# Expert products that read 128 stationary columns where 96 hold tokens

## The reference

```python
def swiglu(h, w1, w3, w2):
    return (jax.nn.silu(h @ w1) * (h @ w3)) @ w2

def moe_swiglu(h, router_w, router_b, w1, w3, w2):
    logits = h @ router_w + router_b
    top_val, top_idx = lax.top_k(logits, 2)
    top_p = jax.nn.softmax(top_val, axis=-1)
    combine = jnp.sum(one_hot(top_idx, 8) * top_p[..., None], axis=-2)
    out = 0
    for e in range(8):
        out = out + combine[..., e:e+1] * swiglu(h, w1[e], w3[e], w2[e])
    return out
```

## Time and profile before

| | |
|---|---|
| median of 3 runs | 2208.56 us (2206.45 to 2208.92) |
| the profiled execution | 2208.2 us, of which the profile's span is 2206.4 us |
| expert stage, first product to last | 1174.3 to 2188.4 us |
| its matmuls | 112 steps x 36 = 4,032 |
| granted clock of TensorE, mean | 0.978 |

### The profile page before, as it was taken

One profiled execution on the slowest core, in us unless ns is written; L12 is line 12 of the kernel. 1 busy time (PEld: TensorE's weight loads), 2 busy tenths in 40 slices (PEclk: granted clock), 3 DMA queues, 4 the chain that ended last, 5 costly groups with the idle time before them and its releaser, 6 DMA issues.

```text
span 2206.4 us, 27500 instructions
## 1 busy us (share of the span) xinstructions
PE 2115.6 (96%) x10750; PEld 1577.5 (71%) x10751; DVE 1121.6 (51%) x1293; ACT 1060.9 (48%) x1163; POOL 1274.9 (58%) x466
## 2 busy tenths in 40 slices
PE   5999999989999998999999999999999999999997
PEld 3875767548787886867986677777767677776775
DVE  2146021140100104354336877878787787888776
ACT  4235411133222124244325766666676666667665
POOL 2300422025445454303406999898989989898996
PEclk8999999989999998999998999999999999999999
DMA  7346323122222222263456999999899999989993
GB/s 301 117 173 267 117 79 131 55 98 77 96 96 95 96 77 96 77 253 147 192 214 232 363 345 345 343 344 363 332 351 345 345 342 345 364 331 353 345 344 135
DMA packets 69640, 503.16 MB, mean 228 GB/s; under 512 B 7744, under 2 KB 7872, under 8 KB 9088
## 3 DMA queue, kind: packets, MB, share of 16 engines
q1 hardware_dynamic: 68976, 497.92, 60.2%
q0 software_dynamic: 528, 3.41, 0.4%
HBM read 500.24 MB, written 1.05 MB: 227 GB/s over the span
## 4 chain that ended last, share of the span: by engine, by line
PE 50%; POOL 33%; issue 12%; ACT 2%; DMA 1%; DVE 1%; SPq 0%; POOLq 0%; ACTq 0%; DVEq 0%
POOL moe_lo L494 32%; PE bank L788 12%; PE bank L789 12%; PE bank L790 12%; PE bank L803 7%; PE bank L820 2%; DMA start_slab<-in_w_mod 1%; PE turned L995 1%; PE pv_bank L1013 1%; POOL w_lo L458 1%; PE bank L971 1%; PE bank L832 1%; ACT PR L1463 0%; ACT H_NEW L1394 0%; POOL HID_LO L726 0%
## 5 line engine op out<-in xcount | busy, mean ns | idle before, releaser
L494 POOL TENSOR_TENSOR moe_lo<-moe_slab,moe_hi 128x512 fp32r<-128x512 f32 x336 | 916.1, 2751 | 163.4 <-ACT moe_hi L1585 162.1
L494 DVE TENSOR_TENSOR moe_lo<-moe_slab,moe_hi 128x1536 fp32r<-128x1536 f32 x336 | 688.4, 2054 | 174.9 <-ACT moe_hi L1585 172.6
L458 POOL TENSOR_TENSOR w_lo<-slab,w_hi 128x2048 fp32r<-128x2048 f32 (+3 forms) x72 | 295.4, 4105 | 678.2 <-ACT w_hi L1351 678.1
L1585 ACT ACTIVATE moe_hi<-moe_slab 128x2048 fp32r<-128x2048 f32 x336 | 629.4, 1906 | 0.1
L788 PE MATMUL bank<-moe_hi,HE_HI 128*96 128x512 f32 x896 | 360.2, 402 | 1.4 <-POOL moe_lo L494 1.4
L790 PE MATMUL bank<-moe_hi,HE_LO 128*96 128x512 f32 x896 | 353.0, 394 | 0.0
L789 PE MATMUL bank<-moe_lo,HE_HI 128*96 128x512 f32 x896 | 351.8, 393 | 0.0
L788 PE MATMUL bank<-H_HI,w_hi 128*128 128x512 f32 (+1 forms) x880 | 325.3, 370 | 17.6 <-POOL H_LO L692 12.6
L789 PE MATMUL bank<-H_LO,w_hi 128*128 128x512 f32 (+1 forms) x880 | 321.6, 365 | 0.0
L790 PE MATMUL bank<-H_HI,w_lo 128*128 128x512 f32 (+1 forms) x880 | 321.0, 365 | 0.0
L1351 ACT ACTIVATE w_hi<-slab 128x2048 fp32r<-128x2048 f32 (+1 forms) x72 | 135.4, 1883 | 161.1 <-PE bank L790 146.3
(11 more groups left out here) (202 smaller groups left out, 2435.8 us busy)
## 6 DMA issues: line engine op xcount, KB each, us to landing
moe_slab<-in_moe_up SPq DMA_DIRECT2D x224, 1024.0 KB, 4.8
moe_slab<-in_moe_w SPq DMA_DIRECT2D x112, 1024.0 KB, 4.9
slab<-in_w_in SPq DMA_DIRECT2D x38, 1024.0 KB, 4.8
slab<-in_ffn_w SPq DMA_DIRECT2D x30, 1024.0 KB, 4.7
slab<-in_w_mod SPq DMA_DIRECT2D x20, 1024.0 KB, 5.4
side_slab<-in_w_mod SPq DMA_DIRECT2D x20, 1024.0 KB, 8.4
start_slab<-in_w_mod SPq DMA_DIRECT2D x8, 1024.0 KB, 17.6
slab<-in_w_proj SPq DMA_DIRECT2D x8, 1024.0 KB, 6.9
```

Source lines behind the costliest of these rows:

```text
L458: engine.tensor_tensor(lo, raw, hi.bitcast(F32), ALU.subtract).then_inc(done, 1)
L494: engine.tensor_tensor(moe_lo[n][:, blocks, :], moe_slab[k % MOE_RING][:, blocks, :], moe_hi[n][:, blocks, :].bitcast(F32), ALU.subtract). ...
L1585: af(moe_hi[k % MOE_SPLIT][:], moe_slab[k % MOE_RING][:], ACT.Copy).then_inc(moe_hi_ready, 1)
```

## The change

The matmuls of the expert products now load 128 stationary columns instead of 96. The window starts where the chunk starts (SLOTS x chunk), so it takes in the chunk's 96 columns and 32 of what lies behind: columns of the next chunk, or, behind the last one, a pad of 32 (WIDE) columns. The result therefore fills all 128 rows of the PSUM bank. Rows 96 to 127 are read by nobody. Moving operands, number of matmuls, and their order stay as they are.

For this HE_HI, HE_LO, GE_HI and GE_LO get another layout, with a pad at the end of each half (HE: 4 chunks and a pad, twice for each expert; GE: 2 chunks and a pad). HE_LO moves to 138.5 KB, GE_HI and GE_LO to 160 and 162, OUT to 16 KB in the ring. The pads are filled with zeros once, by six operations on GpSimd ahead of its first low part of the stage; these wait for `last_turn`, since H and its neighbours lie there until then. TensorE waits for all six (`pads_ready`) behind the first gather. The copies that fill HE and GE handle the same elements in the new layout.

```diff
+WIDE = P - SLOTS
...
-        HE_HI = at("HE_HI", 132, [P, 2, DC, SLOTS], F32R)
-        HE_LO = at("HE_LO", 138, [P, 2, DC, SLOTS], F32R)
+        HE_HI, HE_LO = (at(n, kb_, [P, 2, 2, 4 * SLOTS + WIDE], F32R) for n, kb_ in (("HE_HI", 132), ("HE_LO", 138.5)))
...
-        GE_HI = at("GE_HI", 170, [P, 2, 2, SLOTS], F32R)
-        GE_LO = at("GE_LO", 171.5, [P, 2, 2, SLOTS], F32R)
+        GE_HI, GE_LO = (at(n, kb_, [P, 2, 2 * SLOTS + WIDE], F32R) for n, kb_ in (("GE_HI", 160), ("GE_LO", 162)))
...
-        OUT = at("OUT", 132, [P, DC, S])
+        OUT = at("OUT", 16, [P, DC, S])
...
+            pool.wait_ge(last_turn, 1)
+            for t in (HE_HI, HE_LO):
+                for he in range(2):
+                    nc.gpsimd.memset(t[:, he, :, 4 * SLOTS:].bitcast(F32), 0.0).then_inc(pads_ready, 1)
+            for t in (GE_HI, GE_LO):
+                nc.gpsimd.memset(t[:, :, 2 * SLOTS:].bitcast(F32), 0.0).then_inc(pads_ready, 1)
...
-                    ins = products(up[n % 2][0:SLOTS, :], (HE_HI[:, he, k, :], HE_LO[:, he, k, :]),
+                    ins = products(up[n % 2][:], [t[:, he, half, SLOTS * kk:SLOTS * kk + P] for t in (HE_HI, HE_LO)],
                                    [t[:, kk, :] for t in w], k == 0, k == DC - 1)
...
-                        ins = products(down[half][0:SLOTS, :], (GE_HI[:, n % 2, k, :], GE_LO[:, n % 2, k, :]),
+                        ins = products(down[half][:], [t[:, n % 2, SLOTS * k:SLOTS * k + P] for t in (GE_HI, GE_LO)],
                                        [t[:, 2 * k + half, :] for t in w],
...
             gather(0, (htok_act, htok_dve))
+            pe.wait_ge(pads_ready, 6)
             stream()
...
-                    af(HE_HI[:, he, 4 * b:4 * b + 4, :],
+                    af(HE_HI[:, he, b, 0:4 * SLOTS].rearrange("p (c n) -> p c n", c=4),
                        gath[b][:, 0:4 * SLOTS].rearrange("p (c n) -> p c n", c=4), ACT.Copy).then_inc(he_ready, 1)
```

More of the change, by code:

```diff
@@ L415, in build @@
         onehot_ready, gathered, he_ready = sem("onehot_ready"), sem("gathered"), sem("he_ready")
-        weighted_ready = sem("weighted_ready")
+        weighted_ready, pads_ready = sem("weighted_ready"), sem("pads_ready")
         last_turn, htok_act, htok_dve = sem("last_turn"), sem("htok_act"), sem("htok_dve")
@@ L1570, in turned_hidden @@
                 act.wait_ge(ge_turned, made)
-                af(GE_HI[:, n % 2, :, :], ge_bank[:, 0:2 * SLOTS].rearrange("p (m n) -> p m n", m=2), ACT.Copy)\
+                af(GE_HI[:, n % 2, 0:2 * SLOTS].rearrange("p (m n) -> p m n", m=2), ge_bank[:, 0:2 * SLOTS].rearrange("p (m n) -> p m n", m=2), ACT.Copy)\
                     .then_inc(ge_hi_ready, 1)
@@ L2060, in gathered_out @@
                     dve.wait_ge(he_ready, 2 * n + b + 1)
-                    v.tensor_tensor(HE_LO[:, he, 4 * b:4 * b + 4, :],
+                    v.tensor_tensor(HE_LO[:, he, b, 0:4 * SLOTS].rearrange("p (c n) -> p c n", c=4),
                                     gath[b][:, 0:4 * SLOTS].rearrange("p (c n) -> p c n", c=4),
-                                    HE_HI[:, he, 4 * b:4 * b + 4, :].bitcast(F32), ALU.subtract)\
+                                    HE_HI[:, he, b, 0:4 * SLOTS].bitcast(F32).rearrange("p (c n) -> p c n", c=4), ALU.subtract)\
                         .then_inc(he_lo_ready, 1)
@@ L2067, in turned_hidden @@
                 dve.wait_ge(ge_hi_ready, made)
-                v.tensor_tensor(GE_LO[:, n % 2, :, :], ge_bank[:, 0:2 * SLOTS].rearrange("p (m n) -> p m n", m=2),
-                                GE_HI[:, n % 2, :, :].bitcast(F32), ALU.subtract).then_inc(ge_lo_ready, 1)
+                v.tensor_tensor(GE_LO[:, n % 2, 0:2 * SLOTS].rearrange("p (m n) -> p m n", m=2), ge_bank[:, 0:2 * SLOTS].rearrange("p (m n) -> p m n", m=2),
+                                GE_HI[:, n % 2, 0:2 * SLOTS].bitcast(F32).rearrange("p (m n) -> p m n", m=2), ALU.subtract).then_inc(ge_lo_ready, 1)
             def gated(n, made):
```

## The result

The changed kernel takes 2211.6 us (median of 13 runs, 2210.2 to 2213.7), the kernel before 2207.2 us (13 runs, 2205.6 to 2211.8). The ratio is 1.0019, 95% interval 1.0010 to 1.0027: 2.2 to 6.0 us slower. The forecast was 2195.2 us with a range that began at 2189 and ended at 2204. The time lies outside it, on the other side of no change.

A forecast was written before the change was run, and what follows sets the result against it. TensorE's own queue was taken to bound the expert stage. Gains of 7.1 + 0.8 + 5.6 = 13.5 us, plus 0.1 in the last down product, less 0.3, made 13.3 and a forecast of 2195.2 us, range 2189 to 2204.

The forecast's parts named there:

- the first term: Expert products: reading 128 columns shortens each of 4,032 product distances by 4.6 ns, at most 18.6 us.
- the dense distance: Dense feed-forward, 128 stationary columns: 226.7 ns from product to product, taken as the expert products' new distance instead of 231.3.
- rival 2: Expert products: distance unchanged because it belongs to something else, such as the window's place; 2208.9 us, chance 0.10.
- ten quiet distances: Last down product, other engines finished: ten distances still make 2.31 us, 231 ns each, so load elsewhere doesn't explain them.
- the sum: Whole kernel: 7.1 + 0.8 + 5.6 = 13.5 us gained; 13.3 with the last down product and the start.
- Rival 3: Expert products: more columns make each slower; 24 us more (2233), or 105 more (2313) if the whole load shows; chance 0.05.
- The start: Ahead of the first expert product: fills delay GpSimd's low parts, which meet VectorE's routing; +0.3 us, bounds -0.7 and 3.1.
- rival 4: Start of the expert stage: GpSimd's backlog delays the gather and TensorE's clock returns later; 2 to 5 us, 2199, chance 0.03.
- The covers of a plain step: 47 plain steps of 8.51 us: other engines' slack lets them shrink, 0.02 and 0.03 us left; 0.12 each, 5.6 us.
- rival 1: Plain steps: the chain through other engines takes TensorE's place and they stay at 8.51 us; time 2201, chance 0.14.
- Term (a): 43 steps with extra TensorE work (scatter, gather, turn of the weights): all 36 products count, 7.1 us.
- term (b): 22 steps ended by a chain through other engines: in 15 only 12 products count, 0.8 us; 7 one-hot steps give nothing.

The follow-up runs named there:

- the kernel of 2199.1 us: Against the changed kernel: chunks 512 bytes apart, each with its own pad, and the first product behind each step's transposes reads 96 columns; 2199.1 us, ratio 0.9962.

## Why the prediction was wrong, point by point

**The step that failed** is the first term: "I take the dense distance because every row with 128 columns has it". Those rows had a second thing in common, an address: their chunks follow one another at 128 columns. The prediction saw the difference ("no row shows such a load") and named rival 2 for it, but gave it 0.10, with ten quiet distances at 231 ns as the evidence against. Those ten showed that load elsewhere is not the cause. They could not tell columns from address, since both differ between the groups of the earlier trace rows. The 4.6 ns a product, from which the sum's 13.5 us follow (18.6 at most), were therefore zero here: 233.0 and 230.1 ns by turns in the place of 231.4. Rival 2 is what happened, and its mechanism, the place of a window, is shown by the pair 128 bytes apart. The columns belong to it all the same: at the good place 96 and 112 of them do not get the quick distance (230.2 and 230.5 ns). What rival 2 had wrong is the bound: the place does not only take the gain away, it can cost (232.5 ns).

**A term that was missing** is the load behind the transposes, 112 times 26 ns, about 3 us. The prediction had both records, 162 and 188 ns, and wrote that "both fit under the 231 ns of the product before". Behind two transposes that take 0.33 us together there is no such product. Rival 3 had the price of an exposed load (26 ns), but asked only whether all 4,032 come out or none. For the 112 that do, the Trainium skill, TensorE: Matmul & The Clock Gate, section on LDWEIGHTS, gives the right size: worked out from its rule, 32 columns are an estimate of 27 ns, beside 26 measured.

**The start** was booked at +0.3 us, with bounds of -0.7 and 3.1, and came to +1.2. The fills were cheap, as taken (six in 0.58 us). The mechanism, GpSimd's low parts against VectorE's routing, was named, and rival 4 was its larger form. What failed was the booking of an open sign at nearly zero: three low parts that had run earlier before now run exactly then and cost 1.64 us, and the fourth, which cost 0.69 us before, now costs 1.05. The clock gave 0.8 of these 2.0 us back, where rival 4 expected it to be late.

**What held.** The covers of a plain step: the two thin margins, 0.02 and 0.03 us, were said to let a step shrink to 8.34 us. Once the distance fell, the quickest plain steps shrank to 8.35 and the median to 8.40 (8.39 was expected), so rival 1 did not take over. But the cover is used up: behind the first product of a step, 54 distances in the kernel of 2199.1 us are 245 ns or more (285 in the median), against 16 before. In the 38 that are new the step's first load came late, and GpSimd's low part had ended only 0.15 to 0.19 us ahead of the first product. That costs about 2 us of the stage. The DMA (340 GB/s, 344 in the shortest stage) and the moved OUT showed nothing; OUT was never moved back alone.

**What would have been too much even at the dense distance.** With all windows at a multiple of 256 bytes, and the narrow read behind the transposes, 3.5 ns of the 4.6 come: the stage gains 8.4 us where the sum expected 13.5. Term (a) gave 0.17 us to each of 43 steps, for "the other engines wait for TensorE there". In the medians the scatter steps gained 0.14 us (9.37 to 9.23), the steps with the turn of the weights 0.04 (8.72 to 8.67), and those with a gather nothing (12.04 to 12.05). In these fifteen steps of gather and turn the first load came late (the distance behind the first product is 0.28 to 0.30 us), and behind the gather and the turn stands the exposed load with the slow distances after it. Together they take the gain away. The steps that copy the tokens out, in term (b), even lost 0.05 us (8.85 to 8.90).

**What stays open.** The changed kernel's mean distance (231.4) lies above the mean of the two pure cases (228.5 and 232.5 make 230.5). Windows at a multiple of 256 bytes are slower there (230.1 ns) than in the kernel that has nothing else. Products behind an exposed load were seen to be slower for a while; that a slow window holds up its quick successors in the same way would fit, but isn't shown. The 0.9 us that the layout adds to the stage at 96 columns lies in the distance (231.7 against 231.4 ns) and has no cause either, nor has the 1.2 ns that aligned windows give at 96 columns.

## What to carry to other kernels

A price that is taken from other rows of the same trace is safe only if all their attributes match, and an operand's start address is one: write it down beside the shape before the rows are compared. What paid here (8 us for both together) was to give each stationary chunk 128 columns of its own at a multiple of 256 bytes, with the unused ones padded, and to keep the narrower read where a weight load follows short matmuls and nothing covers it. A wait put in front of work that had slack moves that work: ask what it will run beside when it is let go.

## What the runs showed of the hardware

- Products of 512 columns at full clock follow one another at 226 to 227 ns if their stationary windows have 128 columns (fp32r, 512 bytes) and start at a multiple of 256 bytes, and at 232.5 ns on the mean if they start 128 bytes behind one. At 96 and 112 columns it is 230.2 and 230.5 ns even at multiples of 512 bytes. The Trainium skill, TensorE: Matmul & The Clock Gate, section on weight-path perf modes, says that fast weight load comes on at exactly 128 weights; that 112 columns do not get the quick distance agrees with it. Whether this is that mode no run here can show, since the record of a 128-column load stays at 188 to 189 ns at every place.
- An exposed weight load costs more with more columns: the distance behind the transposes is 285, 303 and 316 ns for 96, 112 and 128 columns. Behind one of 128 columns the next ten distances took 2.30 us where they took 2.27 behind one of 96.
- Small operations on VectorE were held until an instruction of GpSimd ended, by its low parts (0.29 us became 1.31) and by a row of short fills as well (0.86 became 1.38). Not all of them: the reduction at 1161.07, in the middle of a low part, took its 0.29 us as before.
